# Compression taps of 93 columns, gate tiles from step 0, routing rows by identity products, down slabs first

## The reference, cut to what matters

```python
proj = h @ w_in                    # q, k, v, indexer, gates of both attentions
# compressed keys and values of the second attention: 31 blocks of 32 tokens, stride 16
blocks = kv[:, idx] + pe           # pe is a learned offset of each place in a block
kc = silu(blocks.reshape(31, 2, 32 * 64) @ w1) @ w2
# both attentions in blocks of queries: index scores and top-k (dsa), compressed, selected, windowed (nsa)
merged = sigmoid(gate_a) * (o_a @ w_br_a) + sigmoid(gate_b) * (o_b @ w_br_b)
x = x + merged @ w_out
# mixture of experts: 4 groups of 8 experts, the best 2 in the best group for each token
g_logit, e_logit = tok @ w_group + b_group, tok @ w_expert + b_expert
y = sum over the token's 2 experts of weight * ((silu(gate) * up) @ w_down[e])
```

## Time and profile before

| | |
|---|---|
| median of the runs | 2755.05 us |
| the profiled execution's own time | 2757.68 us |
| its span | 2755.8 us |
| TensorE busy | 2615.4 us, 95% |
| VectorE, ScalarE, GpSimd busy | 55%, 38%, 1% |
| mean granted TensorE clock | 0.969 of 2.4 GHz |
| bytes by DMA | 296 MB, 107 GB/s in the mean |

### The profile page before, as it was taken

The page is one execution under the profiler, slowest core; times in us unless marked ns, Lnnn a source line. Parts: engine busy times, 40 slices in busy tenths (PEclk is TensorE's granted clock), DMA queues, the critical chain, the costliest instruction groups (busy, mean ns, idle before and its releaser), DMA issues.

```text
span 2755.8 us, 30114 instructions
## 1 busy us (share of the span) xinstructions
PE 2615.4 (95%) x12106; PEld 1975.0 (72%) x12106; DVE 1528.4 (55%) x2844; ACT 1036.1 (38%) x1779; POOL 25.2 (1%) x27
## 2 busy tenths in 40 slices
PE   8989999979999999899999999989899999999998
PEld 6867677634447566588778888767678888888786
DVE  6357756457767799864354454675533233444534
ACT  5344445321215232334333333257743244432222
POOL 0000000000000000100000000000000000000000
PEclk9889999989999999999999999999999999999999
DMA  4411101299984110213212321212122323123120
GB/s 155 91 37 49 31 32 62 94 397 415 424 355 125 31 31 17 92 68 116 92 67 87 122 92 63 77 61 77 62 92 92 92 62 92 61 77 122 62 92 31
DMA packets 179968, 296.04 MB, mean 107 GB/s; under 512 B 26224, under 2 KB 122992, under 8 KB 171632
## 3 DMA queue, kind: packets, MB, share of 16 engines
q1 hardware_dynamic: 176304, 282.52, 29.5%
q0 software_dynamic: 2304, 8.39, 0.8%
q10 hardware_dynamic: 1216, 3.15, 0.4%
HBM read 288.79 MB, written 4.19 MB: 106 GB/s over the span
## 4 chain that ended last, share of the span: by engine, by line
PE 59%; DVE 5%; ACT 4%; issue 1%; DVEq 0%; ACTq 0%
PE ps L320 16%; PE ps L322 16%; PE ps L321 16%; PE ps L328 7%; PE ps L2142 2%; PE ps L334 1%; PE ps L343 1%; DVE ps L2039 1%; PE ps L2239 1%; PE ps L2169 1%; ACT L2953 0%; PE ps L387 0%; DVE arena L2734 0%; ACT L2971 0%; DVE ws1l L306 0%
## 5 line engine op out<-in xcount | busy, mean ns | idle before, releaser
L306 DVE TENSOR_TENSOR ws0l<-w,ws0h 128x1024 fp32r<-128x1024 f32 (+1 forms) x125 | 135.8, 1086 | 118.9 <-ACT ws0h L298 118.1
L306 DVE TENSOR_TENSOR ws1l<-w,ws1h 128x1024 fp32r<-128x1024 f32 (+2 forms) x125 | 134.9, 1079 | 118.1 <-ACT ws1h L298 118.1
L298 ACT ACTIVATE ws1h<-w 128x1024 fp32r<-128x1024 f32 (+2 forms) x125 | 117.3, 938 | 140.8 <-PE ps L322 135.2
L298 ACT ACTIVATE ws0h<-w 128x1024 fp32r<-128x1024 f32 (+1 forms) x125 | 117.9, 943 | 108.3 <-PE ps L322 105.7
L306 DVE TENSOR_TENSOR ws2l<-w,ws2h 128x1024 fp32r<-128x1024 f32 (+1 forms) x93 | 104.7, 1126 | 93.5 <-ACT ws2h L298 93.5
L2039 DVE SCALAR_TENSOR_TENSOR ps<-arena,ps 128x512 f32<-128x512 f32 x224 | 150.9, 748 | 0.0
L328 PE MATMUL ps<-arena 128*128 128x512 f32 (+11 forms) x440 | 135.3, 483 | 1.6 <-ACT t L765 1.1
L343 PE MATMUL ps<-con,t 128*128 128x128 f32 (+1 forms) x556 | 103.7, 284 | 30.2 <-DVE t L2744 7.3
L320 PE MATMUL ps<-hpc_hi,ws2h 128*128 128x512 f32 x312 | 124.9, 400 | 1.5 <-issue 1.5
L343 PEld LDWEIGHTS ps<-con,t 128*128 128x128 f32 (+1 forms) x556 | 69.1, 141 | 77.8 <-issue 22.6
L320 PE MATMUL ps<-hpc_hi,ws1h 128*128 128x512 f32 x304 | 120.9, 398 | 2.3 <-DVE merged L1169 1.1
(11 more groups left out here) (639 smaller groups left out, 6253.4 us busy)
## 6 DMA issues: line engine op xcount, KB each, us to landing
w<-in_w_gate_up SPq DMA_DIRECT2D x32, 2048.0 KB, 15.4
w<-in_w_in SPq DMA_DIRECT2D x39, 1024.0 KB, 6.2
w<-in_w_down SPq DMA_DIRECT2D x32, 1024.0 KB, 13.4
w<-in_w_ff SPq DMA_DIRECT2D x16, 2048.0 KB, 8.5
w<-in_w_in SPq DMA_DIRECT2D x12, 2048.0 KB, 7.9
w<-in_w_in SPq DMA_DIRECT2D x48, 512.0 KB, 5.3
w<-in_w_branch SPq DMA_DIRECT2D x6, 2048.0 KB, 8.0
w<-in_w_out SPq DMA_DIRECT2D x4, 2048.0 KB, 8.0
```

The source lines that it names most:

```text
L298: A_(e).activation(pair_of(t)[0], tiles[t][1], ACT.Copy).then_inc(*e.inc(hi, ("hi", t)))
L306: e.go.tensor_tensor(p[1], tiles[t][1], p[0].bitcast(F32), ALU.subtract).then_inc(*e.inc(lo, ("lo", t)))
```

## The change

1. **Taps.** The array `z2` moves, and 31 columns are put ahead of it: 30 that need no value and one that holds `pe` (copied there by VectorE, `zpe`). One product of 93 columns does what the products of 62 and 1 did. The places ahead are set to zero at the start of VectorE's program.
2. **Gates.** A table `gate_at` gives the steps. Tile 0 has its parts at steps 0, 0, 1, tile 1 at 3, 4, 5, tile m from 2 on at 6m-5, 6m-3, 6m-1. Tile 0 is split at the end of the first stage, into the pair `wp0`. Tile 1 is split at step 1.
3. **Routing rows.** `spread_columns`: the column itself, repeated 128 times by its access pattern, is the stationary operand, and the identity the moving one, four products of 128 columns for each bank. The weights are worked out before block 0 is placed, and block 0 is placed from the banks in PSUM; the 16 expert counts and `eidi` come after it, then block 1.
4. **Slabs.** The five first down slabs are ahead of all others and wait for the branch products alone. Three gate-up slabs follow, then a wait for the first gather, then the fourth and fifth.

```diff
+            for o, n in ((ZPE[0] - 480, 512), (ZPE[1], 32)):
+                e.go.memset(arena[:, o:o + n], 0.0).then_inc(*e.inc(own_v))
...
+                if g == NG - 2:
+                    e.tile_end = gate_t[0]
+                    act_hi(e, gate_t[0])
...
         def taps(Z, t):
-            v = Z[:, :, t:t + 1]
-            return bass.AP(tensor=v.tensor, offset=v.offset, ap=[v.ap[0], [512, 2], [16, 31]])
+            v = arena[:, ZPE[Z] - 480 + t:ZPE[Z] - 479 + t]
+            return bass.AP(tensor=v.tensor, offset=v.offset, ap=[v.ap[0], [512, 3], [16, 31]])
...
         def cmp_taps_pe(e):
-            e.wait_ge(*in_sw("sw"))
+            e.wait_ge(*dv("zpe"))
...
-                for t in range(16):
-                    e.go.matmul(b[:, 0:62], cmp_v[which][:, t, :], taps(z2[which], 2 * t), start=t == 0, stop=False)
-                    i = e.go.matmul(b[:, 62:63], cmp_v[which][:, t, :], small_w[:, 192 + 16 * which + t:193 + 16 * which + t],
-                                    start=False, stop=t == 15)
+                products(e, ps[4][:, 96 * which:96 * which + 93], [(cmp_v[which][:, t, :], taps(which, 2 * t)) for t in range(16)],
+                         ("taps", which))
...
-        gate_t = [t for c in range(8) for t in stream(4 + c % 2, w1, [(2240 + 256 * c, 256)], ring=(0, 1))]
+        sG, wG = columns(4, w1, [(2240, 256)])
+        tile(sG, wG[:, :, 0:P], 8, (3,))
+        tile(sG, wG[:, :, P:2 * P], 8, (0, 1))
...
+        for m in range(16):
+            for part, t in enumerate(((0, 0, 1), (3, 4, 5))[m] if m < 2 else [6 * m - 5 + 2 * s for s in range(3)]):
+                gate_at.setdefault(t, []).append((m, part))
...
+            def spread_columns(bank, v, key):
+                items = []
+                for i in range(NT):
+                    c = v[:, i:i + 1]
+                    items.append((bank[:, P * i:P * i + P], bass.AP(tensor=c.tensor, offset=c.offset, ap=[c.ap[0], [0, P]]), ident))
+                products_at(e, items, key)
...
             for k in range(2):
-                e.wait_ge(*dv(("slots", k)))
-                products(e, ps[6 + k][:], [(ones, tm[6 + k][:])], ("slots", k))
+                spread_columns(ps[6 + k], posf[:, k, :], ("slots", k))
+            e.wait_ge(*dv("wt2"))
             for k in range(2):
-                e.wait_ge(*dv(("wdiag", k)))
-                products(e, ps[4 + k][:], [(ones, tm[6 + k][:])], ("wrow", k))
+                spread_columns(ps[4 + k], wt2[:, k, :], ("wrow", k))
...
+            e.wait_ge(*dv(("idx", 0)))
+            for k in range(2):
+                e.wait_ge(*mm(("slots", k)))
+                e.go.activation(slot_of[k][:], ps[6 + k][:], ACT.Copy).then_inc(*e.inc(ev, ("slots", k)))
...
+            step(g.tensor_tensor(wt2[:, 1, :], dd, wt2[:, 0, :], ALU.mult), "wt2")
+            place(e, 0)
             for j in range(16):
...
-            for bb in range(2):
-                place(e, bb)
...
+            place(e, 1)
...
+        moe_order = [(h_, 1) for h_ in range(RING)] + [(h_, 0) for h_ in range(RING)]
+        moe_order += [(h_, q) for h_ in range(RING, 2 * NB) for q in range(2)]
...
+                slabs[j].also += [(mm, ("tile", E_END - 1))] if q == 0 else [(mm, ("tile", yE_t[15])), (dv, ("yE", 15))]
...
-            load_slabs(e, M0 + 4)
-            for r in out_row:
-                e.wait_ge(*r("row"))
-            load_slabs(e, M0 + 8)
+            load_slabs(e, M0 + RING + 3)
+            e.wait_ge(*in_xg[0](("x", 0)))
+            load_slabs(e, M0 + 2 * RING)
```

More of the change, by code:

```diff
@@ L636, in p1_dve @@
                     rope(g)
+                if g == 2:
+                    e.wait_ge(*in_sw("sw"))
+                    for which in range(2):
+                        e.go.tensor_copy(zpe[which], small_w[:, 192 + 16 * which:208 + 16 * which]
+                                         ).then_inc(*e.inc(dv, "zpe" if which else None))
                 if g == 6:
                     dve_angles(e, "a1", 1, posf1[:], work[0], work[1])
+            e.tile_end = gate_t[0]
+            dve_lo(e, gate_t[0])
         def p1_pe(e):
@@ L821, in build @@
         G0 = len(slabs)
-        gate_t = [t for c in range(8) for t in stream(4 + c % 2, w1, [(2240 + 256 * c, 256)], ring=(0, 1))]
+        sG, wG = columns(4, w1, [(2240, 256)])
+        tile(sG, wG[:, :, 0:P], 8, (3,))
+        tile(sG, wG[:, :, P:2 * P], 8, (0, 1))
+        slabs[sG].freed = (lo, ("lo", len(tiles) - 1))
+        gate_t = [len(tiles) - 2, len(tiles) - 1]
+        gate_t += [t for c in range(1, 8) for t in stream(4 + c % 2, w1, [(2240 + 256 * c, 256)], ring=(0, 1))]
         for j in (0, 1):
@@ L891, in att1_pe @@
                             score(u)
-                m, s = gate_of(t)
-                if m is not None and s in (0, 2, 4):
-                    if s == 0:
+                for m, part in gate_at.get(t, []):
+                    if part == 0:
                         e.wait_ge(*lo(("lo", gate_t[m])))
@@ L984, in att1_act @@
                     e.go.activation(tm[6][:, 0:n], turns1.bank(("sc", k))[:, 0:n], ACT.Relu).then_inc(*e.inc(ev, ("relu", k)))
[L985 to L988, removed]
+                if t == 1:
+                    act_hi(e, gate_t[1])
+                for m in gate_ends(t):
                     e.wait_ge(*mm(("tile", gate_t[m])))
@@ L1060, in att1_dve @@
                     e.go.tensor_tensor(sv, sv, bc("cmp1", i, 8), ALU.mult).then_inc(*e.inc(dv, ("post", i)))
[L1061 to L1065, removed]
+                if t == 1:
+                    dve_lo(e, gate_t[1])
+                for m in gate_ends(t - 1):
+                    if m + 2 < 16:
+                        dve_lo(e, gate_t[m + 2])
                 if t in fin_at:
@@ L1498, in route_dve @@
             step(g.tensor_tensor(rq, pos, oh2, ALU.mult))
[L1499 to L1504, removed]
+            g.tensor_reduce(posf[:, 0, :], ru, AX, ALU.add).then_inc(*e.inc(own_v))
+            step(g.tensor_reduce(posf[:, 1, :], rq, AX, ALU.add), "posf")
+            e.wait_ge(*ev("gexp"))
+            step(g.tensor_reduce(pg, ga, AX, ALU.add))
+            e.wait_ge(*ev("eexp"))
+            step(g.reciprocal(pg, pg))
+            step(g.tensor_scalar(den, dd, 1.0, None, ALU.add))
+            step(g.reciprocal(den, den))
+            step(g.tensor_tensor(wt2[:, 0, :], den, pg, ALU.mult))
+            step(g.tensor_tensor(wt2[:, 1, :], dd, wt2[:, 0, :], ALU.mult), "wt2")
+            place(e, 0)
             for j in range(16):
@@ L1511, in route_dve, with matched @@
             step(g.tensor_copy(eidi, eidf), "eidi")
-            for bb in range(2):
-                place(e, bb)
[L1515 to L1530, removed]
+            place(e, 1)
+        def matched(e, bb, slots_, row, total):
+            e.go.scalar_tensor_tensor(out=tabs[:, 2, :], in0=slots_, scalar=C("tok")[:, bb:bb + 1], in1=row, op0=ALU.is_equal,
                                       op1=ALU.mult, accum_out=total).then_inc(*e.inc(own_v))
```

57 lines of the change are left out of this document (25 added, 32 removed).

## The result

The changed kernel takes 2741.16 us, the median of 5 runs (2734.32 to 2746.36); the kernel before took 2755.17 beside it. The ratio is 0.9945, with a 95% interval of 0.9928 to 0.9963: 15 us faster, 10 to 20. The forecast was 2731.5, its own range 2727 to 2736, and the range with the rivals ended at 2741 (the ratio times the 2755.05 that the forecast starts from is 2739.9). On two further chips the same kernel gave 2741.55 and 2738.51, with ratios of 0.9929 [0.9908, 0.9950] and 0.9919 [0.9892, 0.9947]; that is 20 and 22 us. The profiled execution is the fastest of the five, 2734.32 with a span of 2732.5, so it flatters the change: 23.3 us against the profile of before, where the medians differ by 14.0.

A forecast was written before the change was run, and what follows sets the result against it. TensorE was busy 95% of the span, so gains lay in removable records, its idle time and low-clock time. Taps 10.2, gates 6.8 and routing 6.5 sum to 23.5 us: 2755.05 to 2731.5, range 2727 to 2736 (2724 to 2741 with rivals (a)-(c)).

The forecast's parts named there:

- Taps: Compression taps: 64 records take 7.3 us, the next slab cuts the saving, next tile at 79.1 not 89.33; 10.2 us gained.
- Gate tiles: Attention: five gate groups move from steps 91 to 99 to steps 0 to 4; 6.8 us gained, between -1.5 and 12.
- Difference nothing: Start of attention: three us more queueing against three less low clock, no net cost; ends 3.5 slower and 2.5 faster.
- if TensorE is at 2.4 GHz all the way: Start of attention: the condition under which gate group 5 ends at 183.3, against 183.2 before.
- Low clock from 171 on, 3.5 slower: Start of attention: the bad end of the range, with TensorE's clock low from 171 us, costing 3.5 us.
- Routing: Routing to the experts' first block: earlier index and a faster first gather start block 0 at 569, not 575.53; 6.5 us gained.
- Rival (a): Routing: the gather is no faster, leaving the routing 2 us; 19 us in all, 2736 us; chance 0.15.
- all is as before: After the experts' first block: nothing else changes, and everything runs 23.5 us earlier.
- rival (b): Attention latency-bound at both ends: start chain delayed, gaps at the end, clock falls at 171; gate edit gives 0; 2738; chance 0.14.
- Rival (c): TensorE stays at 2.4 GHz behind the taps and at attention's start, 2.5 us more at each; 2726.5; chance 0.15.
- Rival (d): The gap behind the taps drops the clock and projections stay at 1.2 GHz, 36 us lost; 2767.5; chance 0.04.
- signs of being wrong: Routing, attention, experts: the gather takes 9 us again, pairs stay over 5 us, or expert blocks begin to wait for slabs.

The follow-up runs named there:

- e6: Changed kernel with the gate groups of attention's steps 0 and 1 behind the index-score product instead of ahead of it: 2735.08 us, ratio 0.9929.
- e12: Changed kernel with index-score products ahead of the gate groups in steps 0 and 1, and two gate-up slabs instead of three before the first gather: 2739.37 us, ratio 0.9917.
- e8: Changed kernel without SyncE's wait for the first gather, so the last two gate-up slabs (4 MB) are asked for at once: 2751.04 us, ratio 0.9974.
- e1: Kernel before with the taps edit alone: 2751.22 us, ratio 0.9970.
- e5: Changed kernel without its gate edit (taps and routing alone): 2745.31 us, ratio 0.9967.
- e10: Changed kernel without its gate edit, run again on another chip: 2740.19 us, ratio 0.9919.
- e3: Kernel before with the routing rows and slab order alone: 2750.47 us, ratio 0.9978.
- e7: Changed kernel with four forms of the taps' moving operand, one run: 0.160, 0.112, 0.112 and 0.169 us a record; no kernel time given.
- e11: Changed kernel without its gate edit, plus 24 unused products of 512 columns behind the index-score products of attention's steps 0 and 1: 2741.42 us, ratio 0.9933.
- e2: Kernel before with the gate edit alone: 2758.91 us, ratio 0.9992.

## Why the prediction was right, and where it was not

**Taps, 10.2 us forecast, 8.9 and then 9.9 in the profile, 8.3 [5.0, 11.9] alone.** The end of the saving was rightly put at the next slab. The price of a record was not: I took the contiguous row of 128 columns, 0.114, for an operand of stride 16, which costs 0.160. The row that would have warned me stood in the trace of before:

```profile
68.16 0.45 PE L698 MATMUL ps<-arena,w 128*128 128x62 f32 x2
68.43 0.32 PE L699 MATMUL ps<-arena,w 128*128 128x1 f32 x2
68.61 0.45 PE L698 MATMUL ps<-arena,w 128*128 128x62 f32 x2
```

From start to start the product of 62 columns takes 0.27 us and that of 1 column 0.18. My "0.11 us whether it has 62 columns or 1" was the mean of 0.135 and 0.09, and it is wrong. The taps became 3.1 us longer than forecast. That this cost nothing, since the slab came later still, was luck. The slab itself landed 1.3 us late, for which no run shows the cause.

**Gate tiles, 6.8 us forecast, 2.2 [-1.7, 6.1] alone, 2.6 between the means of the stage.** This is the step that failed, and in it one half. The pairs are 4.31 us against 4.2 forecast, and the end gives 6.8. The start, which I put at "Difference nothing", costs 3 to 4 us. Group 5 ended at 176.07, where the forecast asks for 173.4 (183.3 less 9.9), 2.7 us late. The chain on which I spent most of the working was nearly right: I had the first transposes at 9.5 us after the first score, and they came at 10.4 (each of the two index-score products costs some 0.7 us, where I had counted 0.3 to 0.4: 156.60, the last gate product ahead of the first, to 157.54, less 0.23), but ScalarE's copies behind them let TensorE go on at 12.8, forecast 12.5. What failed is "if TensorE is at 2.4 GHz all the way": in the profile it stood at 1.2 GHz from 165.3 to 168.7, busy throughout, which is 1.7 of the 2.7 us, and in four of the other changed profiles for 6.8 us. The rest, 0.8, lies in steps 3 to 5. "Low clock from 171 on, 3.5 slower" was in my list as the bad end of the start, and it is near what happened. In e6 and e12, with the index-score product first and the clock at 2.4 GHz, the start costs nothing. The dips in the middle, 3.2 us in the first profile, stood in no case of mine.

**Routing, 6.5 us forecast, 6.0 in the profile, 6.1 [-0.3, 12.7] alone.** The gather went out 25.2 us after the entry, forecast 23.8, and took 4.7 us, forecast 5.3. The index was there at 22.9 after the entry, forecast 23.1, but the stores ended at 24.7 and not at 23.6. Why they ended 1.1 us later behind the same 6 MB is not shown; that slabs ahead of them hold them back is, by e8. The rule of the Trainium skill that the prediction weighed (DMA: Bandwidth & Descriptors, Queues, rings and completion order: each engine takes turns between its queues) speaks for later stores. These traces agree in direction, though none shows the turns themselves. Rival (a), a gather of 8.6 us in an empty queue, is refuted by eleven profiles at 4.5 to 4.9 from issue to block 0.

**The sum.** By block 1 the profiles of the changed kernel have gained 17.4, 16.8 and 18.5 us. That is the forecast less the start of attention (3) and the dips (3). Behind block 1 "all is as before" holds for the work, but the clock's own changes added between -0.3 and 5.9 us in executions of one kernel. The median result lies outside the forecast's own range and at the end of the range with the rivals, 3 us past rival (b)'s 2738, and (b) had part of the reason: the moved groups delay a chain at the start, and the clock falls there. Its other part, gaps at the end, did not occur. Rival (c), the clock holds, came true only in halves: behind the taps in e1, e5 and e10, at the start of attention in e6 and e12. Rival (d) did not occur, and its price was wrong: 72 us of work at 2.4 GHz take 144 at 1.2 GHz, 72 us more and not 36. Of the signs of being wrong that I had named, none came: the gather took 4.7 us, the pairs 4.31, and no expert block waited for a slab. They did not cover the step that failed.

What stays open is why the clock falls near 280 to 300 us in almost every execution with moved gate groups. It fell there in e3 too, which has none. No stretch of idle time there is longer than in the kernel before.

## What to carry to other kernels

When filler products are moved into a stretch where an engine waits, put them behind the short product that starts the chain it waits for, in the same step; two profiles here speak for it, and the medians are too wide to show it. Price a record by a row with the operand's own stride, and take rows of different forms apart before dividing a sum by their number. Before a transfer is put ahead of a dependent one, look at what else is in the queues and unfinished: the victim may be the store that the dependent transfer waits for, not the transfer itself (e8, 9.6 us).

## What the runs showed of the hardware that I had not expected

- An fp32 record of 93 columns takes 0.112 us with a moving operand of stride 1, in one piece or in three, 0.160 with stride 16 and 0.169 with stride 4, all at 2.4 GHz (e7). With stride 16, a record of 62 columns took 0.135 (before).
- The granted clock fell to 1.2 GHz for 13.7 us after 15 us in which TensorE was never idle for more than 0.42 us (e11); ahead of the fall stood 24 wide products and, behind them, small ones of attention. In the kernel before it fell at 73.97, in the middle of the taps of 62 and 1 columns, with TensorE busy throughout. So it did in e2 and e3, with the same taps (72 and 73 us); in the taps of 93 columns it held at 2.4 GHz in all eleven profiles that have them, the four forms of e7 included.
- The same program's stage of attention took 268.9 and 276.2 us in two kernels that differ only behind it (e6, e12). The clock stood at 1.2 GHz for none of the first 265 us in the one and for 17 us in the other: single profiles can't price an edit under 5 us here.
